# A two-layer encoder step with routed experts on one core: the first expert's token rows made by one-hot matmuls from the tiles in the array, and the routing of four tiles placed ahead of the last

## The reference, cut to what matters

```python
def hier_moe(xn, p):
    lg = xn @ p["w_router_group"] + p["b_router_group"]          # 4 groups
    grp = argmax(lg)                                             # one group per token
    le = (xn @ p["w_router_expert"] + p["b_router_expert"]).reshape(B, L, 4, 4)
    le_g = take_along_axis(le, grp)                              # its 4 experts
    top_v, top_i = lax.top_k(le_g, 2)                            # two of them
    w_top = softmax(top_v) * p_grp
    for e in range(16):
        h = silu(xn @ w_exp_gate[e]) * (xn @ w_exp_up[e])
        out = out + combine[..., e:e + 1] * (h @ w_exp_down[e])
```

## Time and profile before

| | us |
|---|---|
| three runs, median | 1418.15 |
| three runs, lowest and highest | 1417.56, 1419.13 |
| the profiled execution, its own time | 1418.4 |
| its span in the trace | 1416.6 |
| busy in the span: TensorE, VectorE, ScalarE, GpSimd | 1355.0, 780.4, 635.7, 114.5 |
| TensorE's mean granted clock in the span | 0.99 of full |

### The profile page before, as it was taken

The page is one execution under the profiler, slowest core; times in us unless marked ns, Lnnn a source line. Parts: engine busy times, 40 slices in busy tenths (PEclk is TensorE's granted clock), DMA queues, the critical chain, the costliest instruction groups (busy, mean ns, idle before and its releaser), DMA issues.

```text
span 1416.6 us, 20810 instructions
## 1 busy us (share of the span) xinstructions
PE 1355.0 (96%) x8342; PEld 1106.7 (78%) x8342; DVE 780.4 (55%) x1151; ACT 635.7 (45%) x932; POOL 114.5 (8%) x96
## 2 busy tenths in 40 slices
PE   7999999999999999999899999999999999999995
PEld 6995666899999767676589857569999988567672
DVE  4425755533335257887663277563433342878866
ACT  5317845422224245656443287562222233465651
POOL 0300000000000010100333000000000000110106
PEclk9999999999999999999999999999999999999998
DMA  8224030023316349998921200303123253799945
GB/s 247 82 86 148 1 120 0 31 90 118 99 50 222 153 162 370 418 409 333 283 83 62 83 0 1 120 1 112 37 89 118 83 200 138 300 405 409 414 179 189
DMA packets 97384, 228.27 MB, mean 161 GB/s; under 512 B 16459, under 2 KB 66661, under 8 KB 84326
## 3 DMA queue, kind: packets, MB, share of 16 engines
q1 hardware_dynamic: 85222, 179.42, 35.2%
q0 software_dynamic: 7904, 32.64, 6.4%
q10 hardware_dynamic: 4176, 15.08, 2.7%
HBM read 198.56 MB, written 33.79 MB: 164 GB/s over the span
## 4 chain that ended last, share of the span: by engine, by line
PE 43%; ACT 2%; DVE 2%; POOL 2%; DMA 1%; issue 1%; ACTq 0%; POOLq 0%; DVEq 0%
PE ps L877 5%; PE ps L879 5%; PE ps L878 5%; PE ps L1396 3%; PE ps L1372 2%; PE ps L1373 2%; PE ps L1374 2%; PE ps L1201 1%; PE ps L903 1%; PE ps L909 1%; PE ps L906 1%; PE ps L1257 1%; PE ps L1259 1%; PE ps L1258 1%; PE ps L1357 1%; PE ps L1057 1%
## 5 line engine op out<-in xcount | busy, mean ns | idle before, releaser
L2007 DVE TENSOR_TENSOR work<-work,ps 128x544 f32<-128x544 f32 x48 | 34.6, 721 | 208.7 <-ACT work L1807 208.7
L1807 ACT ACTIVATE work<-ps 128x544 f32<-128x544 f32 x48 | 30.0, 626 | 244.7 <-PE ps L879 244.7
L782 POOL DMA_INDIRECT rows_back<-xrow_d,row_of x32 | 34.6, 1081 | 1066.9 <-DVE row_of L2443 839.3
L878 PE MATMUL ps<-xn_r,ksv_r 128*128 128x272 f32 x384 | 110.8, 288 | 0.0
L878 PE MATMUL ps<-xn_r,work_r 128*128 128x272 f32 x384 | 110.7, 288 | 0.0
L1374 PE MATMUL ps<-ew_r,rows_tok_r 128*128 128x512 f32 x256 | 99.9, 390 | 0.0
L2007 DVE TENSOR_TENSOR ew_r<-ew,gu_hi_a_r 128x2048 fp32r<-128x2048 f32 x32 | 73.0, 2287 | 17.0 <-ACT gu_hi_a_r L1830 17.0
L878 PEld LDWEIGHTS ps<-xn_r,ksv_r 128*128 128x128 f32 x384 | 72.2, 188 | 0.0
L878 PEld LDWEIGHTS ps<-xn_r,work_r 128*128 128x128 f32 x384 | 72.2, 188 | 0.0
L1830 ACT ACTIVATE gu_hi_a_r<-ew 128x2048 fp32r<-128x2048 f32 x32 | 60.7, 1908 | 5.6 <-ACT yo_b L1877 5.6
L1396 PE MATMUL ps<-ew,acts 128*128 128x512 f32 x128 | 57.9, 595 | 2.5 <-DVE acts L2574 2.5
(11 more groups left out here) (413 smaller groups left out, 3882.5 us busy)
## 6 DMA issues: line engine op xcount, KB each, us to landing
wr<-in_w_in SPq DMA_DIRECT2D x68, 512.0 KB, 4.7
ew<-in_w_exp_gate SPq DMA_DIRECT2D x32, 1024.0 KB, 7.2
ew<-in_w_exp_up SPq DMA_DIRECT2D x32, 1024.0 KB, 11.0
ew<-in_w_exp_down SPq DMA_DIRECT2D x32, 1024.0 KB, 10.2
wr<-in_w_out SPq DMA_DIRECT2D x16, 512.0 KB, 4.4
rows_d<-yo_a ACTq DMA_DIRECT2D x14, 512.0 KB, 8.1
rows_d<-yo_b ACTq DMA_DIRECT2D x14, 512.0 KB, 8.3
rows_d<-in_zeros POOLq DMA_DIRECT2D x10, 512.0 KB, 9.4
```

The lines of the kernel that those rows point to most:

```text
L782: pool.indirect_dma_start(xg[:, e % 2, :], None, xrow_d, bass.IndirectOffsetOnAxis(ap=row_of[:, e:e + 1], axis=0)).then_inc(xg_in[e % 2][0 ...
L878: mm(out_[h], w_hi, x_lo[:, c], start=False, stop=False, skip_group_check=True)
L1807: f(halves(sg[:, v % 2, :]), banks(4 * (v % 2)), ACT.Sigmoid).then_inc(br_sg[0], 1)
L2007: return v_.tensor_tensor(o_, a, b, op)
```

## The change

Expert 0 no longer goes through DRAM. `MID` makes tile 0 the last tile. The logits of tiles 4, 1, 2 and 3 are finished one k step earlier and ranked by VectorE (`ranks(1, NTILE)`) before it adds the last tile's half; tile 0 is ranked alone afterwards (`ranks(0, 1)`). The places within an expert are counted in the order of tiles 1, 2, 3, 4 and then 0 (`counts_early`, `counts_late`). VectorE writes expert 0's one-hot tables in float32 into `rows_back` (`hot_first`), and TensorE multiplies the normalised rows of each tile, which stand in the array, with that tile's table (`first_rows`): eight matmuls per tile accumulate expert 0's rows, already transposed, in banks 2 and 3. GpSimd gathers experts 1 to 15. The row numbers and transposes of the next experts, ScalarE's copies of expert 1's weights and VectorE's subtractions move to other places in their queues, and all but one of the `busy` groups in this stretch go. `oh_rdy`, `rk_mm` and `xg_in` count accordingly.

```diff
@@ -28,7 +28,7 @@
-MID = [4, 0, 1, 2, 3]
+MID = [4, 1, 2, 3, 0]
@@ -76,9 +76,10 @@
+LG_BANK = [4, 4, 4, 4, 7]
@@ -247,6 +248,7 @@
+        hot_first = moe["rows_back"][:, 0:NTILE * P].rearrange("p (t n) -> p t n", t=NTILE)
@@ -695,8 +697,7 @@
-                for s in range(2):
-                    sp.wait_ge(xg_in[s][0], at(xg_in[s], l, 16))
+                sp.wait_ge(xg_in[1][0], at(xg_in[1], l, 16))
@@ -783,7 +784,7 @@
-                for e in range(NE):
+                for e in range(1, NE):
@@ -1311,7 +1312,7 @@
-                        if p == last and k == 6:
+                        if p == last and k == 5:
@@ -1321,24 +1322,50 @@
-                busy(7, 1, 256)
+                def counts_early():
+                    pe.wait_ge(oh_rdy[0], at(oh_rdy, l, 1))
+                    pe.wait_ge(dve_fills[0], DVE_FILLS + 5)
+                    mm(ps[:, 5, 16:80], stri_b[:, :], oh_b[:, 16:80], start=True, stop=False, skip_group_check=True)
+                    for j in range(1, NTILE - 1):
+                        n = NTILE - 1 - j
+                        ins = mm(ps[:, 5, 16 * (j + 1):80].rearrange("p (t e) -> p t e", t=n), ones_b[:, :],
+                                 oh_b[:, 16 * j:16 * j + 16].unsqueeze(1).to_broadcast([P, n, NE]),
+                                 start=False, stop=(j == NTILE - 2), skip_group_check=True)
+                    ins.then_inc(rk_mm[0], 1)
+                def counts_late():
+                    pe.wait_ge(oh_rdy[0], at(oh_rdy, l, 3))
+                    for j in range(1, NTILE):
+                        mm(ps[:, 4, 100:132].rearrange("p (t e) -> p t e", t=2), ones_b[:, :],
+                           oh_b[:, 16 * j:16 * j + 16].unsqueeze(1).to_broadcast([P, 2, NE]), start=(j == 1), stop=False, skip_group_check=True)
+                    mm(ps[:, 4, 100:116], stri_b[:, :], oh_b[:, 0:16], start=False, stop=False, skip_group_check=True)
+                    mm(ps[:, 4, 116:132], ones_b[:, :], oh_b[:, 0:16], start=False, stop=True, skip_group_check=True).then_inc(rk_mm[0], 1)
+                def first_rows(t):
+                    m = TM[t]
+                    if t == 1:
+                        pe.wait_ge(oh_rdy[0], at(oh_rdy, l, 2))
+                        pe.wait_ge(fn_x[0], at(fn_x, l, NTILE - 1))
+                    if t == 0:
+                        pe.wait_ge(hot_rdy[0], at(hot_rdy, l, 1))
+                        pe.wait_ge(fn_x[0], at(fn_x, l, NTILE))
+                    if m < P:
+                        stand(pe)
+                    for k in range(DC):
+                        ins = mm(bank(2 + k // 4, P, P, P * (k % 4)), by_residue(xrow[t][0:m, :])[:, k, :], hot_first[0:m, t, :],
+                                 start=(t == 1 and k % 4 == 0), stop=(t == 0), skip_group_check=True)
+                    return ins
-                busy(7, 1, 256)
+                counts_early()
-                busy(7, 3)
...
-                ins.then_inc(rk_mm[0], 1)
+                first_rows(1)
+                counts_late()
+                first_rows(2)
+                first_rows(3).then_inc(idx_mm[0], 1)
@@ -1351,7 +1378,7 @@
-                        pe.wait_ge(xg_in[s][0], at(xg_in[s], l, (n - s) * 8 + 16))
+                        pe.wait_ge(xg_in[s][0], at(xg_in[s], l, (n - s) * 8 + 16 * s))
@@ -1407,21 +1434,21 @@
-                busy(6, 1)
-                row_numbers(0, 7, 0)
+                row_numbers(1, 7, 2)
+                first_rows(4)
+                first_rows(0).then_inc(xg_tr[0], 1)
+                row_numbers(2, 7, 4)
-                row_numbers(1, 7, 2)
-                busy(6, 2)
-                row_numbers(2, 7, 4)
-                busy(6, 4)
-                turn_rows(0, 0)
-                busy(6, 2)
-                row_numbers(3, 7, 6)
-                busy(6, 1)
+                def second_rows():
+                    row_numbers(3, 7, 6)
+                    turn_rows(1, 1)
-                    gate_up(e, e % 2, SLOT[e], between=(lambda: turn_rows(1, 1)) if e == 0 else None)
+                    gate_up(e, e % 2, SLOT[e], between=second_rows if e == 0 else None)
@@ -1852,6 +1879,8 @@
+                act.wait_ge(rt_mm[0], at(rt_mm, l, NTILE))
+                weights_high(1, 1, 1, 0, (0, 1))
@@ -1863,7 +1892,8 @@
-                    f(xg_hi[s].rearrange("p (b k) n -> p b k n", b=2), ps[:, 0:2, :].rearrange("p b (k n) -> p b k n", k=4), ACT.Copy).then_inc(xg_up[0], 1)
+                    b = 2 if isinstance(n, int) and n == 0 else 0
+                    f(xg_hi[s].rearrange("p (b k) n -> p b k n", b=2), ps[:, b:b + 2, :].rearrange("p b (k n) -> p b k n", k=4), ACT.Copy).then_inc(xg_up[0], 1)
@@ -1893,8 +1923,7 @@
-                act.wait_ge(rt_mm[0], at(rt_mm, l, NTILE))
-                weights_high(1, 1, 1, 0, (0, 1))
+                act.wait_ge(spill[0], at(spill, l, 16 + 16 * NTILE))
@@ -2374,18 +2403,67 @@
...
+                def ranks(a, b):
+                    n = 5 * (b - a)
+                    lg, bt = groups(r_lg)[:, 5 * a:5 * b], beats[:, 5 * a:5 * b]
+                    link(tt(bt, lg.unsqueeze(2).to_broadcast([P, n, 4, 4]), lg.unsqueeze(3).to_broadcast([P, n, 4, 4]), ALU.subtract))
+                    link(tt(bt, bt, tie[:, 0:n], ALU.is_gt))
+                    link(v_.tensor_reduce(groups(r_rank)[:, 5 * a:5 * b], bt, AX, ALU.add))
+                    link(v_.scalar_tensor_tensor(out=r_og[:, a:b], in0=rank_g[:, a:b], scalar=0.0, in1=valid[:, a:b], op0=ALU.is_equal, op1=ALU.mult))
+                    chosen(oh_b[:, 0:80], 1.5, ALU.is_lt, a, b).then_inc(oh_rdy[0], 1)
+                def places_of(a, b, counted):
+                    return v_.scalar_tensor_tensor(out=r_sel[:, a:b].rearrange("p t e -> p (t e)"), in0=counted, scalar=1.0, in1=oh_b[:, 16 * a:16 * b],
+                                                   op0=ALU.add, op1=ALU.mult)
+                def first_hot(a, b):
+                    return tt(hot_first[:, a:b, :], iota.unsqueeze(1).to_broadcast([P, b - a, P]), r_sel[:, a:b, 0].unsqueeze(2).to_broadcast([P, b - a, P]),
+                              ALU.is_equal)
+                    if p == NTILE - 1:
+                        dve.wait_ge(rt_mm[0], at(rt_mm, l, p))
+                        for i in range(p - 1):
+                            biased(i, MID[i])
+                        link(biased(p - 1, MID[p - 1]))
+                        ranks(1, NTILE)
-                    if p == NTILE - 1:
-                        for i in range(p):
-                            biased(i, MID[i])
-                        dve.wait_ge(fn_tr[0], at(fn_tr, l, p + 2))
-                        b = 2 * (p % 2) + 1
-                        v_.tensor_copy(xnT[p % 2][:, 4:8, :], ps[:, b, :].rearrange("p (k n) -> p k n", k=4)).then_inc(fn_ev[0], 1)
-                    scaled(p, t, xrow[t], gain_ffn, frs, fn_rs, fn_x)
+                    if p < NTILE - 1:
+                        scaled(p, t, xrow[t], gain_ffn, frs, fn_rs, fn_x)
+                dve.wait_ge(fn_tr[0], at(fn_tr, l, NTILE + 1))
+                v_.tensor_copy(xnT[0][:, 4:8, :], ps[:, 1, :].rearrange("p (k n) -> p k n", k=4)).then_inc(fn_ev[0], 1)
+                dve.wait_ge(rk_mm[0], at(rk_mm, l, 1))
+                link(places_of(1, NTILE, ps[:, 5, 16:80]))
+                first_hot(1, NTILE).then_inc(oh_rdy[0], 1)
+                link(biased(NTILE - 1, MID[NTILE - 1]))
+                ranks(0, 1)
+                scaled(NTILE - 1, MID[NTILE - 1], xrow[MID[NTILE - 1]], gain_ffn, frs, fn_rs, fn_x)
+                dve.wait_ge(rk_mm[0], at(rk_mm, l, 2))
+                dve.wait_ge(oh_rdy[0], at(oh_rdy, l, 3))
+                places_of(0, 1, ps[:, 4, 100:116]).then_inc(sel_rdy[0], 1)
+                dve.wait_ge(sel_rdy[0], at(sel_rdy, l, 1))
+                first_hot(0, 1).then_inc(hot_rdy[0], 1)
@@ -2394,36 +2472,13 @@
...
-                chosen(oh_b[:, 0:80], 1.5, ALU.is_lt).then_inc(oh_rdy[0], 1)
...
@@ -2431,9 +2486,12 @@
-                one_hot(0)
-                chosen(oh12[:, 1], 1.0, ALU.is_equal)
-                link(v_.tensor_copy(r_cnt, ps[:, 5, 0:96]))
+                one_hot(1)
+                chosen(oh12[:, 0], 0.0, ALU.is_equal, 0, NTILE)
+                link(chosen(oh12[:, 1], 1.0, ALU.is_equal, 0, NTILE))
+                v_.tensor_copy(r_cnt[:, 16:80], ps[:, 5, 16:80]).then_inc(idx_ev[0], 1)
+                v_.tensor_copy(r_cnt[:, 0:16], ps[:, 4, 100:116])
+                link(v_.tensor_copy(r_cnt[:, 80:96], ps[:, 4, 116:132]))
@@ -2451,12 +2509,11 @@
-                row_number(0, 7, 0)
-                one_hot(1)
+                rows_low(0, 0)
@@ -2573,9 +2624,8 @@
-                rows_low(0, 0)
+                row_number(3, 7, 6)
-                row_number(3, 7, 6)
```

59 lines of the change are left out of this document (19 added, 40 removed).

## The result

The forecast was wrong, in its sign too. The changed kernel takes 1435.74 us (median of 4 runs, 1433.89 to 1439.2), the kernel before took 1418.64 in the same set: ratio 1.012, with a 95% interval of 1.0099 to 1.014. The profiled execution took 1434.14 us, with a span of 1432.2 (before: 1418.4 and 1416.6) and a mean grant of 0.982 (before 0.99). The loss is small, 1.2%, but clear of the noise.

The account below looks back on a forecast made before the run. TensorE was taken to bound the expert loop, so only the routing chain ahead could be won: -5.8 and -2.8 us, plus 1.5 for the clock, -7.1 from 1418.4; median forecast 1411.1 us, range 1407.5 to 1416.6.

Parts of the forecast that it names:

- TensorE from 513.0: Products forming expert 0's rows on TensorE: 80 records at 0.11 us, 8.8 us per layer, bounds 8.6 and 10.7.
- rival (c): Slower: the 80 records run at half clock, 17.0 us per layer; +7.9, 1426.3 us; decides from 0.164 a record; chance 0.07.
- Tile 4 priced as a full tile: In expert 0's row products, tile 4's 32 rows of weights cost a full tile; otherwise 1.3 us shorter per layer.
- Ranking hidden, VectorE free at 509.4: Ahead of the last half tile's addition: ranking four tiles fits VectorE's wait until 509.80, 0.4 us to spare.
- Expert 1 waits for VectorE, a stand of 1.3 to 1.9 us: Before expert 1's matmuls, TensorE stands 1.3 to 1.9 us for VectorE's queue; expert 1 starts at 533.85.
- Expert 0's down products lose their wait of 0.51 us: At expert 0's down matmuls: the 0.51 us wait for VectorE goes, 0.5 us gained per layer.
- One fall of the clock in four places, +1.5: Two thin or idle TensorE places per layer, from 509.8 to 513.0 and at 532: one fall of four, +1.5 us.
- rival (a): The clock falls at three or four of the four places: -2.6 us in sum, 1415.6 us; chance 0.14.
- Sum of -8.6 us: Gain ahead of the expert loop before clock cost: -5.8 us in layer 0, -2.8 in layer 1.
- Rival (b): The expert loop is really bound by transfers and gives the earlier start back: 1418 us; chance 0.08.

Follow-up runs that it names:

- contig: Changed kernel with 128 adjacent columns as stationary operand in the products forming expert 0's rows, in place of every eighth (feature order wrong, for timing only): 1419.28 us.
- early_only: Changed kernel with expert 0's rows gathered from DRAM again; four tiles still ranked ahead, tile 0 still last: 1427.77 us.
- r_tail: r_clock with VectorE's queue ahead of expert 1 reordered: first weight half before expert 3's row numbers, expert 1's rows before its second weight half: 1415.71 us.
- s_late: r_tail with TensorE's thin work of the last two tiles in four pieces and expert 2's second weight half after expert 0's activation copy: 1413.4 us, ratio 0.9951.
- r_clock: resmajor with the first thin batch of logits and transposes issued after two projection groups, not three, and fillers around the last transposes and logits: 1418.07 us.
- t_late: r_tail with the second half of expert 2's weight remainders made after VectorE's copy of expert 0's activations: 1415.67 us.
- step2: Changed kernel with that stationary operand read in steps of two elements (8 bytes) instead of eight (feature order wrong, for timing only): 1422.64 us.
- step4: Changed kernel with that stationary operand read in steps of four elements (16 bytes) instead of eight (feature order wrong, for timing only): 1436.42 us in one execution.
- fills: Changed kernel with ten fillers of 256 columns put back on TensorE, from the last projection to the second group of expert 0's row products: 1444.76 us.
- resmajor: Changed kernel, computation whole, with scaled rows written in the other feature order so that all stationary operands are adjacent: 1419.79 us.

## Why the prediction was wrong

- *TensorE from 513.0, "I take 0.11 ... 8.8 us, with bounds 8.6 and 10.7".* This step failed: 20.30 us. Both bounds came from rows whose operand was adjacent, the logits and the transposes in the earlier trace rows; the step of 32 bytes stood in the quoted source and I priced only the columns. With this step a load takes 336 ns instead of 192. With adjacent operands the price would have been fair: 2.05 + 3.82 + 2.05 + 2.05 = 9.97 us in sum, at 0.119 from one record to the next. By the forecast's own formula in rival (c), 160 x (0.247 - 0.11) - 8.6 = +13.3, 1431.7 us; the profiled execution was 1434.1.
- *Rival (c), TensorE's own path, from 0.164 a record on.* The right path, with the wrong cause: it took the half clock for the condition, and the mean grant of 0.99 then spoke against it. Its threshold counted on all else coming true: contig, with (3.51 + 3.82 + 2.05 + 2.05) / 80 = 0.143 a record in layer 0, was already no faster than before. Its chance of 0.07 was too low for a form that "no row has".
- *Tile 4 priced as a full tile.* Right: 4.18 us beside 4.15 in the changed kernel, 2.05 beside 2.05 in contig.
- *Ranking hidden, VectorE free at 509.4.* Right: the last operation of the four tiles' ranks ended at 508.08, and the addition began at 509.99. But that it takes the scaling and the store back, which early_only prices, I had seen only for expert 2's load.
- *Expert 1 waits for VectorE, a stand of 1.3 to 1.9 us.* Right in kind, 2.10 in both layers, and right about VectorE. I hadn't asked how much of that queue was mere order: r_tail moved the stand and s_late removed it, with a few lines in another order.
- *Expert 0's down products lose their wait of 0.51 us.* Right, the row at 552.03 has none.
- *One fall of the clock in four places, +1.5.* Too few: the changed kernel shows four, and contig's layer 0 alone three, about 5 us, one of them in the projection, which was not among my places. The price of one, 1.5 to 1.8 us, was right where the clock bounds the records, and 0.28 us where their loads do. So rival (a) holds on top of (c).
- *Sum of -8.6 us.* As a potential it was fair: r_clock and r_tail start expert 2 5.5 and 2.4 us earlier than before, -7.9. But they are only 1.6 and 3.8 us faster in the median, and where the rest goes is read in part only.
- *Rival (b), the loop bound by transfers.* Rejected because TensorE was busy 20.00 of 20. That shows who bounds the loop now, not how much the other has in reserve. In the traces contig's lead of 2.3 us passes through layer 0's loop whole, and t_late's of 6.4 comes out as 1.0.

## What to carry to other kernels

Look at the step of a stationary operand before pricing its products, not only at its shape: with 16 bytes or more between FP32 elements each of these loads took 0.33 instead of 0.19 us, and a layout written once by another engine can give it back (here 16 us for 0.85 to 1.1 us per tile on VectorE). When a form has no row in the trace, its bounds must come from rows that differ in one thing at a time, and its chance of surprise belongs in the range. After a large term is won, ask what has just that much in reserve: here the order of VectorE's queue, then, as far as the traces tell, the transfers of the loop. And before a trace explains a median, set its own time beside it: t_late's was 6.1 us above.

## What the runs showed of the hardware

- Loads of 128x128 FP32 stationary operands: 192 ns adjacent, 196 in steps of 8 bytes, 329 in steps of 16 and 336 in steps of 32 (medians of contig, step2, step4 and the changed kernel). Between a grant of 0.50 and of 1.00, 16 records bound by them differ by 0.28 us (4.15 in the changed kernel, 3.87 in fills).
- In transposes the loads are 138 to 143 ns adjacent (resmajor) and 185 to 226 in steps of 32 bytes (the kernel before), and eight transposes take 1.09 and 1.14 us.
- VectorE's scaling with both inputs in steps of 32 bytes and the output adjacent (resmajor): 2.13 to 2.39 us for 128x1024, against 1.28 in the kernel before.
- TensorE counts as fully busy in records that only wait for their weights (4.00 of 4.00 us from 513.30 to 517.30 above), and was granted 0.50 of its clock there and 1.00 in the same work from 521.50 to 525.20.
